# Unnormalised attention weights with one late scaling per head pair, in a fused decoder layer

## The reference, cut to what matters

```python
score = jnp.einsum('bqhk,bqh->bqk', rel, wib)          # indexer, then top 256 keys of each query
_, idx = lax.top_k(score, k_top)
logits = jnp.einsum('bqhd,bqkhd->bhqk', qb, kg) * (D_HEAD ** -0.5)
logits = jnp.where(sel_ok[:, None], logits, -jnp.inf)
p = jax.nn.softmax(logits, axis=-1)
o_ds = jnp.einsum('bhqk,bqkhd->bqhd', p, vg)
merged = gate_sb * (o_sb @ w_branch_sb) + gate_ds * (o_ds @ w_branch_dsa)
```

## Time and profile before

| | |
|---|---|
| median of 3 runs | 1851.16 us (1847.76 to 1852.23) |
| profiled execution, own time | 1850.96 us |
| its span, first to last instruction | 1849.2 us |
| TensorE matmul busy | 1763.0 us (95%) |
| VectorE busy | 1022.0 us (55%) |
| ScalarE busy | 703.3 us (38%) |
| GpSimd busy | 398.4 us (22%) |
| DSA half, first score matmul to the branch block's first matmul | 743.90 to 947.50 us |

### The profile page before, as it was taken

The page is one execution under the profiler, slowest core; times in us unless marked ns, Lnnn a source line. Parts: engine busy times, 40 slices in busy tenths (PEclk is TensorE's granted clock), DMA queues, the critical chain, the costliest instruction groups (busy, mean ns, idle before and its releaser), DMA issues. The chain is left out here.

```text
span 1849.2 us, 25696 instructions
## 1 busy us (share of the span) xinstructions
PE 1763.0 (95%) x10056; PEld 1497.1 (81%) x10056; DVE 1022.0 (55%) x1764; ACT 703.3 (38%) x1375; POOL 398.4 (22%) x174
## 2 busy tenths in 40 slices
PE   3999999999999999899999899999999999999998
PEld 3989888899878878788878688888888888888886
DVE  5277788999999997576744244322222222222225
ACT  5256444444444444699941232302121121203032
POOL 1112222221111111111014510404041222314033
PEclk6999999999999999899999899999999999999999
DMA  4565424424323423444124432202020211112023
GB/s 133 172 187 147 134 74 131 140 85 111 112 68 96 114 67 102 104 95 100 42 103 139 169 114 91 91 12 80 12 80 22 70 41 51 51 41 71 21 75 142
DMA packets 65584, 170.55 MB, mean 92 GB/s; under 512 B 9320, under 2 KB 23976, under 8 KB 65464
## 3 DMA queue, kind: packets, MB, share of 16 engines
q1 hardware_dynamic: 65464, 168.91, 30.3%
HBM read 126.47 MB, written 42.41 MB: 91 GB/s over the span
## 5 line engine op out<-in xcount | busy, mean ns | idle before, releaser
L606 PE MATMUL bk<-x_hi,w_hi 128*128 128x512 f32 (+2 forms) x832 | 308.6, 371 | 6.3 <-PEq L284 6.3
L606 PE MATMUL bk<-x_lo,w_hi 128*128 128x512 f32 (+2 forms) x832 | 298.2, 358 | 0.0
L606 PE MATMUL bk<-x_hi,w_lo 128*128 128x512 f32 (+2 forms) x832 | 297.6, 358 | 0.0
L265 POOL TENSOR_TENSOR w_lo<-w_raw,w_hi 128x1024 fp32r<-128x1024 f32 x53 | 131.3, 2479 | 483.9 <-ACT w_hi L261 483.8
L1382 ACT ACTIVATE relu<-bank 128x1024 f32<-128x1024 f32 x32 | 32.9, 1029 | 504.7 <-PE bank L1293 504.7
L1293 PE MATMUL bank<-m_hi,w_hi 128*128 128x512 f32 x512 | 199.5, 390 | 0.0
L1293 PE MATMUL bank<-m_hi,w_lo 128*128 128x512 f32 x512 | 199.2, 389 | 0.0
L1293 PE MATMUL bank<-m_lo,w_hi 128*128 128x512 f32 x512 | 199.2, 389 | 0.0
L947 DVE TENSOR_SCALAR_CACHE_REDUCE sel<-sc,st_bits 128x272 bf16<-128x272 f32 (+6 forms) x217 | 184.2, 890 | 0.9
L606 PEld LDWEIGHTS bk<-x_hi,w_hi 128*128 128x128 f32 x832 | 158.7, 191 | 22.1 <-POOL w_lo L265 6.4
L1463 DVE TENSOR_TENSOR acc<-acc,bank 128x1024 f32<-128x1024 f32 x56 | 68.3, 1220 | 192.6 <-PE bank L1269 191.7
(11 more groups left out here) (177 smaller groups left out, 3586.1 us busy)
## 6 DMA issues: line engine op xcount, KB each, us to landing
w_raw<-w_units SPq DMA_DIRECT2D x99, 512.0 KB, 3.7
raw<-w_units SPq DMA_DIRECT2D x24, 512.0 KB, 3.5
k_hi<-k_d SPq DMA_DIRECT2D x32, 260.0 KB, 5.3
k_lo<-k_d SPq DMA_DIRECT2D x32, 260.0 KB, 5.9
q_st<-q_d SPq DMA_DIRECT2D x32, 256.0 KB, 4.7
g_d<-stage_hi SPq DMA_DIRECT2D x32, 256.0 KB
gate<-g_d SPq DMA_DIRECT2D x16, 512.0 KB, 4.4
v_raw<-v_d SPq DMA_DIRECT2D x16, 260.0 KB, 7.2
```

Source lines behind the costliest of these rows:

```text
L265: pool.tensor_tensor(w_lo[:, s], w_raw[:, s], w_hi[:, s].bitcast(F32), ALU.subtract).then_inc(lo_done, 1)
L606: mm = pe.matmul(pj[b][:, 0:c1 - c0], w[:, s, kt, :], a[:, kt, c0:c1], start=kt == 0 and k == 0, stop=kt == KT - 1 and k == 2)
```

## The change

The exponentials are no longer normalised: L785 and L1034 go, and `turn` waits for the exponent alone. Each exponent leaves its row sum in a column of its own in `small`, 16 columns for each pair of heads. Once a pair's 16 sums are there (steps 80, 96, 112, 128), VectorE runs one reciprocal that reads each of the 16 columns 64 times (stride 0) and writes 128x1024 (`r_wide`). TensorE transposes it in eight 128x128 tiles into two PSUM banks of the ring that `turn` uses (steps 83, 99, 115, 129). VectorE multiplies the pair's raw outputs in place by the two banks (`scale_pair`); then ScalarE and GpSimd round and subtract as before. For the fourth pair VectorE copies the two banks to `r_last`, and the multiplication, the rounding and the subtraction stand at the start of the branch block, where TensorE waits for them ahead of row tile 7 of unit 0. Its raw outputs use the ordinary `output` copy; L819 and L1057 go. The `scale_pair` comes behind `rest_weights` and `rest_values` in VectorE's step.

```diff
@@ attention: schedule
+PAIR_AT = [NJ // 2 + 16 * (p_ + 1) + 3 for p_ in range(3)] + [NJ + 1]
+    if j_ in PAIR_AT:
+        for half_ in range(2):
+            tp_take(("r", PAIR_AT.index(j_), half_), j_)
@@ TensorE
 def turn(j):
-    pe.wait_ge(a_done, j + 1)
+    if t == SB:
+        pe.wait_ge(a_done, j + 1)
+    else:
+        pe.wait_ge(exp_done, j + 1 - NJ // 2)
+def turn_sums(p):
+    pe.wait_ge(recip, p + 1)
+    for half in range(2):
+        n = TPN["r", p, half]
+        turn_bank(n)
+        for m in range(4):
+            i = 4 * half + m
+            mm = pe.transpose(bk[TP_BANK[n]][:, m * P:(m + 1) * P], r_wide[:, i * P:(i + 1) * P], idf[:])
+        mm.then_inc(tp_ready, 1)
@@ in the loop, after turn and values
+    if j in PAIR_AT:
+        turn_sums(PAIR_AT.index(j))
@@ ScalarE
-def normalise(j):
-    act.wait_ge(recip, j - NJ // 2 + 1)
-    act.activation(a, a, ACT.Copy, scale=small[:, 24 + s:25 + s]).then_inc(a_done, 1)
 def round_pair(p):
-    act.wait_ge(o_free, STEPS + 16 * (p + 1))
-    act.copy(o_hi[:, 4 + p, :], o_pair[:, p, :]).then_inc(op_hi, 1)
+    act.wait_ge(tp_free, TPN["r", p, 1] + 1)
+    act.copy(o_hi[:, 4 + p, :], o_pair[p][:]).then_inc(op_hi, 1)
@@ VectorE
-def normalise(j):
-    dve.wait_ge(exp_done, e + 1)
-    if e >= 2:
-        dve.wait_ge(a_done, j - 1)
-    dve.reciprocal(small[:, 24 + s:25 + s], small[:, 20 + j % 4:21 + j % 4]).then_inc(recip, 1)
+def reciprocals(p):
+    dve.wait_ge(exp_done, 16 * (p + 1))
+    sums = small[:, 128 + 16 * p:144 + 16 * p]
+    if p:
+        dve.wait_ge(tp_ready, TPN["r", p - 1, 1] + 1)
+    dve.reciprocal(r_wide[:].rearrange("p (c d) -> p c d", d=DH), sums.unsqueeze(2).broadcast_to([P, 16, DH])).then_inc(recip, 1)
+def scale_pair(p):
+    if p < 3:
+        dve.wait_ge(o_free, NJ // 2 + 16 * (p + 1))
+    else:
+        dve.wait_ge(or_lo, 4)
+    for half in range(2):
+        dve.wait_ge(tp_ready, n + 1)
+        if p < 3:
+            dve.tensor_tensor(o_pair[p][:, cols], o_pair[p][:, cols], src, ALU.mult).then_inc(tp_free, 1)
+        else:
+            dve.tensor_copy(r_last[:, cols], src).then_inc(tp_free, 1)
-def rest_output(j):
-    dve.wait_ge(oh_done, j + 1 - PAIRED)
-    dve.tensor_tensor(o_lo[dst], bk[o_bank(j)][0:DH, 0:P], o_hi[dst].bitcast(F32), ALU.subtract).then_inc(o_free, 1)
@@ in the loop, at its start, ahead of logits(j)
+    if j > NJ // 2 and j % 16 == 0:
+        reciprocals((j - NJ // 2) // 16 - 1)
@@ branch block: TensorE, ScalarE, VectorE
-mm = unit_mm(pe, u % 2, o_hi, o_lo, outs, kts=range(4 * t, 4 * t + 4))
+mm = unit_mm(pe, u % 2, o_hi, o_lo, outs, kts=range(4 * t, 4 * t + 4),
+             before=lambda kt: pe.wait_ge(last_lo, 1) if k == 0 and kt == KT - 1 else None)
+act.wait_ge(last_mul, 1)
+act.copy(o_hi[:, KT - 1, :], o_pair[3][:]).then_inc(last_hi, 1)
+dve.tensor_tensor(o_pair[3][:], o_pair[3][:], r_last[:], ALU.mult).then_inc(last_mul, 1)
+dve.wait_ge(last_hi, 1)
+dve.tensor_tensor(o_lo[:, KT - 1, :], o_pair[3][:], o_hi[:, KT - 1, :].bitcast(F32), ALU.subtract).then_inc(last_lo, 1)
```

More of the change, by code:

```diff
@@ L106 @@
 NZ_SB = Z_END[NJ // 2 - 1]
+RELOAD = [NJ // 2 + 6 + 10 * p_ for p_ in range(4)]
+PAIR_AT = [NJ // 2 + 16 * (p_ + 1) + 3 for p_ in range(3)] + [NJ + 1]
 TPN, TP_BANK = {}, []
@@ L125 @@
             tp_take(("v", j_ // NB + 1, half_), j_)
+    if j_ in PAIR_AT:
+        for half_ in range(2):
+            tp_take(("r", PAIR_AT.index(j_), half_), j_)
+R_GROUPS = sorted(n_ for key_, n_ in TPN.items() if key_[0] == "r")
+HI_NO = [n_ - sum(r_ < n_ for r_ in R_GROUPS) for n_ in range(len(TP_BANK))]
 TP_PREV = [max([m_ for m_ in range(n_) if TP_BANK[m_] == b_], default=None) for n_, b_ in enumerate(TP_BANK)]
@@ L180 @@
 SEARCH[SEARCH_STEPS] = [1e8, 0.0]
-RELOAD = [STEPS + 6 + 10 * p_ for p_ in range(4)]
-PAIR_AT = [STEPS + 16 * (p_ + 1) + 3 for p_ in range(3)]
-PAIRED = STEPS + 48
 O_W = 16512
@@ L411, in build @@
         o_st = at("o_st", [DH, 2, P], F32, O_OST)
-        o_pair = at("o_pair", [P, 3, SEQ], F32, O_SC)
+        o_pair = [at(f"o_pair{p}", [P, SEQ], F32, O_SC + 4096 * p if p < 3 else O_STAGE) for p in range(4)]
+        r_wide = at("r_wide", [P, SEQ], F32, O_SC + 3 * 4096)
+        r_last = at("r_last", [P, SEQ], F32, O_STAGE + 4096)
         sc = at("sc", [P, STOT], F32, O_SC)
@@ L446, in build @@
             tp_ready, tp_hi, tp_free = sem("f_tp"), sem("f_tphi"), sem("f_tpfree")
-            pv_done, o_free, oh_done = sem("f_pv"), sem("f_ofree"), sem("f_oh")
+            pv_done, o_free = sem("f_pv"), sem("f_ofree")
             o_spilled = [sem("f_ospill0"), sem("f_ospill1")]
@@ L450, in build, with sum_col @@
             op_hi, op_lo, mask_done = sem("f_ophi"), sem("f_oplo"), sem("f_mask")
+            def sum_col(j):
+                t, g, i = JOBS[j]
+                return 128 + 16 * ((g - H) // 2) + 2 * i + g % 2
             block = st.enter_context(nc.Block())
@@ L583, in _ @@
                             pool.wait_ge(op_hi, p + 1)
-                            pool.tensor_tensor(o_lo[:, 4 + p, :], o_pair[:, p, :], o_hi[:, 4 + p, :].bitcast(F32), ALU.subtract).then_inc(op_lo, 1)
+                            pool.tensor_tensor(o_lo[:, 4 + p, :], o_pair[p][:], o_hi[:, 4 + p, :].bitcast(F32), ALU.subtract).then_inc(op_lo, 1)
             @block.tensor
@@ L778, in exponent @@
                     act.activation(a_buf[:, j % 3, 0:keys], n_buf[:, s, 0:keys], ACT.Exp, scale=-1.0, bias=small[:, 16 + s:17 + s],
-                                   accum_out=small[:, 20 + j % 4:21 + j % 4]).then_inc(exp_done, 1)
-                def normalise(j):
-                    keys, s = KEYS[JOBS[j][2]], j % 2
-                    a = a_buf[:, j % 3, 0:keys]
-                    act.wait_ge(recip, j - NJ // 2 + 1)
-                    act.activation(a, a, ACT.Copy, scale=small[:, 24 + s:25 + s]).then_inc(a_done, 1)
+                                   accum_out=small[:, sum_col(j):sum_col(j) + 1]).then_inc(exp_done, 1)
                 def round_weights(j):
@@ L811, in output @@
                         act.copy(o_st[:, j % 2], bk[o_bank(j)][0:DH, 0:P]).then_inc(o_free, 1)
-                    elif j < PAIRED:
-                        r = DH * (g % 2)
+                    else:
+                        r, p = DH * (g % 2), (g - H) // 2
                         if j == NJ // 2:
                             act.wait_ge(mask_done, 1)
[L816 to L819, removed]
+                        if j == NJ // 2 + 48:
+                            act.wait_ge(or_lo, 3)
+                        act.copy(o_pair[p][r:r + DH, i * P:(i + 1) * P], bk[o_bank(j)][0:DH, 0:P]).then_inc(o_free, 1)
                 def round_pair(p):
-                    act.wait_ge(o_free, STEPS + 16 * (p + 1))
-                    act.copy(o_hi[:, 4 + p, :], o_pair[:, p, :]).then_inc(op_hi, 1)
+                    act.wait_ge(tp_free, TPN["r", p, 1] + 1)
+                    act.copy(o_hi[:, 4 + p, :], o_pair[p][:]).then_inc(op_hi, 1)
                 def reload(p):
@@ L841, in _ @@
                         evacuate(n)
-                    if 1 <= j < NJ + 1 and JOBS[j - 1][0] == DS:
-                        normalise(j - 1)
                     if 2 <= j < NJ + 2:
@@ L1022, in logits @@
                             dve.wait_ge(zd_used, z - NZ_SB)
-                        out = small[:, 16 + s:17 + s] if c1 == keys else small[:, 18 + m:19 + m]
+                        out = small[:, 16 + s:17 + s] if c1 == keys else small[:, 24 + 2 * s + m:25 + 2 * s + m]
                         dve.tensor_tensor_reduce(n_buf[:, s, c0:c1], bk[2 + z % 2][:, 0:c1 - c0], sel[:, BOFF[i] + c0:BOFF[i] + c1],
@@ L1026, in logits @@
                         last = out
-                def normalise(j):
-                    t, g, i = JOBS[j]
-                    s, e, keys = j % 2, j - NJ // 2, KEYS[i]
-                    dve.wait_ge(exp_done, e + 1)
-                    if e >= 2:
-                        dve.wait_ge(a_done, j - 1)
-                    dve.reciprocal(small[:, 24 + s:25 + s], small[:, 20 + j % 4:21 + j % 4]).then_inc(recip, 1)
+                def reciprocals(p):
[10 more added lines that the diff above has]
+                    for half in range(2):
+                        n = TPN["r", p, half]
+                        src, cols = bk[TP_BANK[n]][:], slice(half * HALF, (half + 1) * HALF)
+                        dve.wait_ge(tp_ready, n + 1)
+                        if p < 3:
+                            dve.tensor_tensor(o_pair[p][:, cols], o_pair[p][:, cols], src, ALU.mult).then_inc(tp_free, 1)
+                        else:
+                            dve.tensor_copy(r_last[:, cols], src).then_inc(tp_free, 1)
                 def rest_weights(j):
@@ L1039, in rest_weights @@
                         n, m = TPN["p", j, k], len(tiles)
-                        dve.wait_ge(tp_hi, n + 1)
+                        dve.wait_ge(tp_hi, HI_NO[n] + 1)
                         dst = (slice(None), j % 2, slice(4 * k, 4 * k + m), slice(None))
@@ L1047, in rest_values @@
```

(17 more changed lines are left out.)

## The result

| | before | after |
|---|---|---|
| median | 1849.57 us (4 runs) | 1873.17 us (4 runs, 1871.75 to 1874.12) |
| ratio | | 1.0118, 95% interval 1.0099 to 1.0137 |
| span of the profiled execution | 1849.2 us | 1871.5 us |
| DSA half up to the branch block | 203.6 us | 224.9 us |

The change makes the kernel slower by 1.2%: its median is 22.2 us over the profiled execution of before, where 30 us more (1881 us) were forecast. (The two medians alone give a ratio of 1.0128, inside the interval; the four runs of before lie apart, two near 1848 and two at 1851 and 1852.) The DSA half explains 21.3 of the 22.3 us between the spans. It also begins 1.2 us later, where nothing was changed.

What follows compares the result with a forecast made beforehand. TensorE's own work was taken as 92% of the DSA half's middle, ScalarE delaying it indirectly. Terms -12.7 + 2.6 + 0.9 + 23.6 + 6.7 + 9.6 = +30.7 us on 1850.96 gave 1881 us; own range 1868 to 1893, eight in ten 1841 to 1892.

Steps and rivals of the forecast that it cites:

- The forecast case: Whole kernel: the wide reciprocal is paid per column and stalls TensorE; 1881 us, chance 0.58.
- multiplications gone, middle: Steps 72 to 126: without ScalarE's multiplications and VectorE's small reciprocals, 70% of 12.4 us returns, 8.7 us.
- tail without the wide reciprocal: Step 127 to the branch block: 8.5 us instead of 11.64, a gain of 3.1 us, bounds 0 and 4.
- one wide reciprocal, D: VectorE, 1024 columns, four times: 8.3 us each at 8 ns excess per column, bounds 1.2 and 19.6.
- its stall in the three steps: Steps 80, 96, 112: the third score chunk waits for the reciprocal, 7.85 us each, 23.6 us in all.
- tail with it: From step 128: the last jobs wait for the reciprocal; block end at 15.2 us instead of 8.5, 6.7 us lost.
- lowered clock: Behind four new idle stretches of TensorE: 2.4 us lost each, 9.6 in all, bounds 0 and 12.
- the 12.4 us: Steps 72 to 126: time that ScalarE, VectorE and the clock add to TensorE's own 146.2 of 158.6 us.
- A: Wide reciprocal runs at one column a cycle, 1.2 us instead of 8.3; kernel 1844 us, chance 0.22.
- B: Reciprocal quick, but the middle's excess is small semaphore gaps, only a fifth returns; no change, 1851 us, chance 0.10.
- C: A middle reciprocal of 4.3 us by the 4 ns reading; kernel 1863 us, chance 0.07.
- D: As a rival: the upper reading, a wide reciprocal of 19.6 us; kernel 1927 us, chance 0.03.

Runs made afterwards that it cites:

- narrow version: The changed kernel, but the reciprocal takes 16 columns and a plain VectorE copy spreads them to the 1024 of r_wide; 1839.23 us, ratio 0.9938 to before.

## Why the prediction was right, and which terms were off

The forecast case was the one that came: slower, by the width of the reciprocal, through the third score chunk. The measured 1873 us lie in its own range of 1868 to 1893. The terms of its sum against the runs:

| term | forecast, us | measured, us |
|---|---|---|
| multiplications gone, middle | -8.7 (0 to -12.4) | -11.2 in the run without them; -12.5 with the fourth pair moved too (narrow version, 149.88 less 2.6 of transposes and 3 x 0.4 of longer waits) |
| first steps | -0.9 | -0.3 (33.38 to 33.09) |
| tail without the wide reciprocal | 8.5 long | 8.83 long (narrow version) |
| 24 transposes | +2.6 | +2.6 (3 x 0.88) |
| scaling | +0.9 | 0 (steps 84, 85 at their shortest) |
| one wide reciprocal, D | 8.3 | 6.55 |
| its stall in the three steps | 3 x (D - 0.45) = 23.6 | 3 x 5.9 = 17.7 (6.33 less the 0.42 of any such step) |
| tail with it | +6.7 | +7.2 over the narrow version |
| lowered clock | +9.6 for four | 9.4 for the middle's three alone, some 2 more in the tail |

**The term that was mis-sized is D, the length of one wide reciprocal.** It was put between the two smaller excesses of a one-column reciprocal, at 8 ns a column. The chip needs 254 ns for 16 columns, 542 for 64 (median) and 6553 for 1024; (6553 - 254) / 1008 is 6.25 ns a column. The formula around it held: D - 0.45 gives 6.1 for the 5.9 measured. That the excess is paid per column at all was an assumption from differences of 4 to 19 ns, and 8 ns was a choice between two readings that differ by more than twice; that it came so near is partly luck. With the measured D the three steps would have been forecast at 18.3 and the tail at 5.0, 7 us less in all, 1875 us instead of 1881.

The Trainium skill's "VectorE: DVE Perf Modes", section "First, the fixed hardware budget", gives the reciprocal a repeat count of 8; with the 0.96 GHz of its section "Specifications" the estimate is 8.3 ns a column. The runs give 6.25 ns, which would be 6.0 cycles of that clock; the measurement decides. The trace agrees with a repeated operation in so far as 1024 columns of a reciprocal take 6553 ns and 1024 of an ordinary pass 1225. Why it is this figure, no run shows.

**The other errors.** The multiplications were worth more than the 70% that were assumed: in the narrow version every step between 72 and 126 that has neither a reciprocal nor the new transposes is at its shortest. With the fourth pair moved all of the 12.4 us came back. That makes the forecast too high by 3.8 us, on the same side as D. The scaling adds 0.9 to it. Only the clock works against them. It cost about the forecast sum in the middle alone: of each step like 80 (10.85 us) 3.35 is its shortest length and 5.9 the longer wait, which leaves 1.6 us, three times, and steps 81, 82, 97 and 98 are 4.6 us over their shortest, at a clock of 0.50 in step 81; behind step 112 nothing is lost. The tail's share is on top: 7.2 us against the 5.0 that D alone gives. So the forecast's even 2.4 us for each stall was not what happened (3.5, 4.3 and 1.6 in the middle), though the sum came near. The measured terms add up to 21.3 us (-12.5 - 0.3 - 2.8 + 2.6 + 17.7 + 7.2 + 9.4), which is what the half grew by.

**Rivals.** A, a reciprocal at a column a cycle, is what the narrow version builds by other means; its 1844 us were too cautious by 5 (1839.23 measured). B, no gain from the multiplications, is refuted by the run without them (12.2 us). C and D are excluded by the measured 6.55 us.

**The signs named ahead:** four reciprocals of 7 to 10 us: missed, 6.55. Waits of 7 us or more in steps 80, 96, 112: missed, 6.33. Lowered clock behind each: so in two of the three, while after the third it rose again at the end of step 112. Ordinary heads at 21.5 to 22.5 us: 21.3, even better. ScalarE near 65% of the half: 58% (16.27 + 108.26 + 5.21 = 129.7 of 224.9 us). No wait ahead of row tile 7: right. In the middle ScalarE fell by 37 us and not by the 43.4 of the multiplications: in the kernel before, ScalarE's records add up to 166 us for 145.5 us of busy time, so they overlap.

## What to carry to other kernels

In this kernel an instruction's cost on a half idle engine went by the longest unbroken piece, and not by the sum of the pieces: 34.4 us of VectorE time in pieces of 0.54 us cost 28 us less than 26.2 us in four. Compute a slow function at the width of its distinct values and spread the result with a copy. Price an operation at a new shape from its own row at the old shape, and look for a difference to its neighbours there: here 4 to 19 ns in one column were the only sign of 6.4 us.

## What the runs showed of the hardware

VectorE's reciprocal takes 6.25 ns a column in float32; a copy that repeats each of 16 columns 64 times takes 0.69 us for 1024 on VectorE and 1.04 us on GpSimd. In three waits of TensorE of 6.3 us each the clock fell to 1.2 GHz before the wait was over, and it stayed there for 8, 9.5 and 4 us behind it, so that a stall costs more than its length: in the kernel before with four idle reciprocals 34.7 us for 26.1 us.
